# Recurrent stage of a hybrid decoder step: paired products in four quarters of the array, the next pair's preparation moved

## The reference, cut to what matters

```python
decay = jnp.exp(-jnp.exp(w_log))                       # w_log from tanh(xw) @ w_decay
a = jax.nn.sigmoid(a0 + xa @ w_aaa)
kk = k * k_k
k = k * (1.0 + (a - 1.0) * k_a)
kk = kk / jnp.maximum(jnp.sqrt(jnp.sum(kk * kk, axis=-1, keepdims=True)), 1e-12)
a_vec, b_vec = -kk, kk * a_h

def step(S, inp):
    r_t, w_t, k_t, v_t, av_t, bv_t = inp
    sa = jnp.einsum('bhvk,bhk->bhv', S, av_t)
    S = S * w_t[:, :, None, :] + sa[..., None] * bv_t[:, :, None, :] + v_t[..., None] * k_t[:, :, None, :]
    return S, jnp.einsum('bhvk,bhk->bhv', S, r_t)

out = (groupnorm(y) * lnx_w + lnx_b + bonus) * g       # bonus = sum(r * k * r_k) * v
```

## Time and profile before

| | us |
|---|---|
| median of 3 runs | 2424.03 (2423.95 to 2425.92) |
| profiled execution | 2424.27 |
| its span | 2422.6 |
| recurrent stage (550 to 1148 of the span), of it | 598 |
| TensorE busy there | 588.5 |
| VectorE busy there | 398.1 |
| ScalarE busy there | 193.1 |

### The profile page before, as it was taken

How to read it: one execution, slowest core, us unless ns; L and a number is a source line. 1 busy time by engine, 2 the same in 40 slices (tenths; PEclk the granted TensorE clock), 3 DMA queues, 4 the chain that set the end, 5 groups by cost and what they waited for, 6 DMA issues and landing times.

```text
span 2422.6 us, 48639 instructions
## 1 busy us (share of the span) xinstructions
PE 2375.1 (98%) x19616; PEld 2272.0 (94%) x19616; DVE 1461.7 (60%) x2052; ACT 895.2 (37%) x1040; POOL 131.4 (5%) x203
## 2 busy tenths in 40 slices
PE   8999999999999999999999998999999999999998
PEld 6899999898988889888999988999999999999998
DVE  5645544555677666776544446666666666666676
ACT  6443344343333333332434344333333333333334
POOL 3000001000000010000000001000000000000003
PEclk9999999999999999999999999999999999999999
DMA  7554487342333333323444632444444444444443
GB/s 267 185 162 145 156 290 244 104 141 83 96 98 95 93 126 100 97 86 95 142 150 151 202 121 89 158 154 139 156 156 140 154 150 144 140 158 153 152 143 110
DMA packets 282189, 346.67 MB, mean 143 GB/s; under 512 B 6957, under 2 KB 240733, under 8 KB 280907
## 3 DMA queue, kind: packets, MB, share of 16 engines
q1 hardware_dynamic: 271883, 307.66, 39.6%
q0 software_dynamic: 9712, 36.30, 4.5%
q10 hardware_dynamic: 464, 0.79, 0.1%
HBM read 333.83 MB, written 10.89 MB: 142 GB/s over the span
## 4 chain that ended last, share of the span: by engine, by line
PE 86%; DVE 8%; issue 3%; ACT 2%; DMA 1%; DVEq 0%; SPq 0%; ACTq 0%
PE bank L246 20%; PE bank L247 20%; PE bank L255 20%; PE bank L1165 5%; PE bank L227 4%; PE bank L228 4%; PE bank L229 4%; DVE work L906 1%; ACT hi L211 1%; DVE lo L218 1%; PE bank L1181 1%; PE bank L511 1%; DVE q L833 1%; PE bank L512 1%; PE bank L518 1%
## 5 line engine op out<-in xcount | busy, mean ns | idle before, releaser
L218 DVE TENSOR_TENSOR lo<-raw,hi 128x2048 fp32r<-128x2048 f32 x286 | 655.6, 2292 | 505.5 <-ACT hi L211 488.0
L246 PE MATMUL bank<-ah,hi 128*128 128x320 f32 x3200 | 958.0, 313 | 0.2 <-DVE al L532 0.2
L247 PE MATMUL bank<-al,hi 128*128 128x320 f32 x3200 | 945.8, 309 | 0.0
L211 ACT ACTIVATE hi<-raw 128x2048 fp32r<-128x2048 f32 x286 | 548.0, 1916 | 924.1 <-PE bank L255 675.4
L246 PEld LDWEIGHTS bank<-ah,hi 128*128 128x128 f32 x3200 | 600.7, 188 | 12.9 <-issue 9.8
L247 PEld LDWEIGHTS bank<-al,hi 128*128 128x128 f32 x3200 | 601.1, 188 | 0.4
L255 PE MATMUL bank<-ah,lo 128*128 128x320 f32 x3200 | 546.6, 311 | 0.0
L255 PEld LDWEIGHTS bank<-ah,lo 128*128 128x128 f32 x3200 | 486.4, 188 | 3.7 <-issue 0.8
L227 PE MATMUL bank<-bh,hi 128*128 128x320 f32 x704 | 218.7, 311 | 0.2 <-DVE work L2314 0.2
L229 PE MATMUL bank<-bh,lo 128*128 128x320 f32 x704 | 217.6, 309 | 0.0
L228 PE MATMUL bank<-bl,hi 128*128 128x320 f32 x704 | 217.5, 309 | 0.0
(11 more groups left out here) (377 smaller groups left out, 2035.7 us busy)
## 6 DMA issues: line engine op xcount, KB each, us to landing
raw<-in_w_in SPq DMA_DIRECT2D x98, 1024.0 KB, 5.3
raw<-in_w_up SPq DMA_DIRECT2D x88, 1024.0 KB, 5.1
raw<-in_w_down SPq DMA_DIRECT2D x44, 1024.0 KB, 5.1
raw<-in_w_branch SPq DMA_DIRECT2D x24, 1024.0 KB, 5.4
raw<-in_w_out SPq DMA_DIRECT2D x16, 1024.0 KB, 5.5
raw<-in_w_mem_k SPq DMA_DIRECT2D x8, 1024.0 KB, 5.5
raw<-in_w_mem_v SPq DMA_DIRECT2D x8, 1024.0 KB, 5.3
work<-in_cache_mem_k POOLq DMA_DIRECT2D x8, 1024.0 KB, 6.0
```

The costliest lines, as they stand in the source:

```text
L211: act.activation(hi[c % NS][:, :], raw[c % 2][:, :], ACT.Copy).then_inc(S("hi_done"), 1)
L218: dve.tensor_tensor(lo[c % NS][:, :], raw[c % 2][:, :], hi[c % NS][:, :], ALU.subtract)\
L246: pe.matmul(out, w, xh[:, 8 * h + k, :], start=h + k == 0, stop=False)
L247: pe.matmul(out, w, xl[:, 8 * h + k, :], start=False, stop=False)
```

## The change

- Products with inputs of both kinds are made two at a time in one pass over chunks (`both`): A with B, beT with Cb, Bk with Ck, vT with kaT. Chunks 0 and 1 (`TURNED`) send head 0 to partitions 64 to 127 and head 1 to 0 to 63, in one bank; chunks 2, 3 and 4 (`UPRIGHT`) stay, in a second bank. Their matmuls alternate. The products that follow read the turned halves through `out_of_chunk`.
- G and the first two terms of S0 to S3 become St and Ss, made together; S1 to S3 keep the one term with the state before, and VectorE adds the rest while it copies out. X is split in X1 and X. The terms of y of chunks 0 and 1 are made beside S4.
- bonus and ssq come first in the pair. bonus is copied out by ScalarE and multiplied later by VectorE; the root of ssq is taken by ScalarE from PSUM, and the bound on the norm becomes the `min` of `prepare_norm`. `prepare_kk` is done a pair ahead.
- z and za stand behind vks, ahead of RT2. On VectorE prepare_norm comes ahead of RT2, prepare_k behind it, prepare_logs behind Z1, branch(0, 1) behind the copy of y, weights_low(4) behind prepare_rest.
- `STEPS` puts the 48 branch steps in other places, and `HELD` replaces `Y_STEPS`: four are within alT, three ahead of y.

```diff
-        for _n in ["A", "bonus", "B", "beT", "Cb", "A2", "B2", "Bk", "vT", "RT1", "B4", "Ck", "kaT", "RT2", "s0t",
-                   "Q", "QT", "Z0", "Z0s", "Q2", "QT2", "XB", "Z1", "QT4", "alT", "Z2", "z", "za", "ssq", "Z3", "X4", "G",
-                   "S0", "S1", "S2", "S4", "S3", "X", "g", "mean", "trp", "var", "tr0", "tr1"]:
+        for _n in ["bonus", "ssq", "ABt", "ABs", "beCt", "beCs", "A2", "B2", "BCt", "BCs", "RT1", "B4", "vkt", "vks", "z", "za", "RT2", "s0t",
+                   "Q", "QT", "Z0", "Z0s", "Q2", "QT2", "XB", "Z1", "QT4", "alT", "Z2", "Z3", "X4", "St", "Ss",
+                   "S1", "X1", "S2", "S4", "S3", "X", "g", "mean", "trp", "var", "tr0", "tr1"]:
...
-        STEPS = {"A": 8, "A2": 3, "RT1": 3, "RT2": 3, "Q": 3, "XB": 3, "Z2": 4, "Z3": 4, "S0": 2, "S1": 2, "S2": 2, "S3": 1, "X": 2,
+        STEPS = {"bonus": 8, "A2": 3, "RT1": 3, "RT2": 3, "Q": 3, "XB": 3, "alT": 4, "Z3": 4, "S1": 3, "S2": 3, "S3": 3,
                  "g": 5, "mean": 2, "var": 1}
-        Y_STEPS = 3
+        HELD = {"alT": 4, "g": 3}
...
-                masked(t_ad, "A", m_ad)
-                ps("bonus")
-                tt(bon, pbank("bonus")[:, 0:T], row_(i + 16), ALU.mult, "ring_out")
-                masked(t_bd, "B", m_bd, None)
-                tt(c5(t_bo)[:, 0:NCK], c5(pbank("B")[:, 0:T])[:, 0:NCK], bmid(m_bo[:, :], NCK), ALU.mult, "ring_out")
-                ps("beT")
-                vv.do(dve.tensor_copy(zc3[:, :, 0:64], c5(pbank("beT")[:, 0:T])), "ring_out")
-                ps("Cb")
-                tt(zc3[:, :, 64:128], c5(pbank("Cb")[:, 0:T]), m_in[:, :, :], ALU.mult, "ring_out")
...
+                for name, cs in (("ABt", TURNED), ("ABs", UPRIGHT)):
+                    k, states = 64 * len(cs), tuple(c for c in cs if c < NCK)
+                    ps(name)
+                    part(t_ad, name, 0, cs, m_ad)
+                    part(t_bd, name, k, cs, m_bd)
+                    part(t_bo, name, k, states, m_bo, "ring_out")
+                for name, cs in (("beCt", TURNED), ("beCs", UPRIGHT)):
+                    k = 64 * len(cs)
+                    ps(name)
+                    vv.do(dve.tensor_copy(zc3[:, cs[0]:cs[-1] + 1, 0:64], c3(pbank(name)[:, 0:k])))
+                    tt(zc3[:, cs[0]:cs[-1] + 1, 64:128], c3(pbank(name)[:, k:2 * k]), m_in[:, cs[0]:cs[-1] + 1, :], ALU.mult, "ring_out")
...
+                dve.wait_ge(S("turned_out"), OUT0_A + N_OUT_A * i + OUT_A["bonus"] + 1)
+                tt(bon, bon, row_(i + 16), ALU.mult)
+                prepare_norm(dve, vv, i + 1)
                 plus(t_rt, "RT2")
-                prepare_kk(dve, vv, i + 1)
+                prepare_k(dve, vv, i + 1)
...
+                ps("X1")
+                tt(t_x[:, 64:128], t_x[:, 64:128], pbank("X1")[:, 0:64], ALU.add, "ring_out")
+                state(2)
                 branch(0, 0)
-                state(2)
                 weights_low(3)
                 ps("S4")
                 tt(sam, pbank("S4")[:, :].rearrange("p (b v) -> p b v", b=NB), s0t, ALU.add)
                 tt(sam, sam, bc(pend_s, HD), ALU.mult, "ring_out")
                 state(3)
-                branch(0, 1)
                 ps("X")
-                tt(t_x[:, 64:TP], t_x[:, 64:TP], pbank("X")[:, 0:192], ALU.add, "ring_out")
-                prepare_norm(dve, vv, i + 1)
-                weights_low(4)
+                tt(t_x[:, 128:TP], t_x[:, 128:TP], pbank("X")[:, 0:128], ALU.add, "ring_out")
                 prepare_al(dve, vv, i + 1)
                 dve.wait_ge(S("y_ps"), i + 1)
                 vv.do(dve.tensor_copy(y_, bank[6][:, 0:T]), "y_out")
+                branch(0, 1)
                 prepare_rest(dve, vv, i + 1)
+                weights_low(4)
...
+                ps("bonus")
+                act.wait_ge(S("gated_out"), j)
+                aa.do(act.activation(bon, pbank("bonus")[:, 0:T], ACT.Copy), "turned_out")
+                ps("ssq")
+                aa.do(act.activation(sq, pbank("ssq")[:, 0:T], ACT.Sqrt), "kk_root")
+                for name, c, k in (("vkt", 0, 128), ("vks", 128, 192)):
...
+            if ps:
+                ps("s0t")
+                aa.do(act.activation(qr[:, 896:1408], pbank("s0t")[:, :], ACT.Copy), "turned_out")
+                ps("alT")
+                aa.do(act.activation(alp_t[:, 0:192], pbank("alT")[:, 0:192], ACT.Copy), "turned_out")
             act.wait_ge(S("logs"), j + 1)
...
+                def into_chunk(o, a, b, c):
+                    for h in range(2):
+                        last = pe.matmul(o[half(h ^ (c in TURNED)), :], a[half(h), :], b[half(h), :], start=True, stop=True)
+                    return last
+                def out_of_chunk(o, a, b, c, start=True, stop=True, **kw):
+                    for h in range(2):
+                        r = half(h ^ (c in TURNED))
+                        last = pe.matmul(o[half(h), :], a[r, :], b[r, :], start=start, stop=stop, **kw)
+                    return last
+                def both(turned, upright, a1, b1, a2, b2):
+                    t, s = begin(turned), begin(upright, ahead=1)
+                    if turned == "ABt":
+                        wait("ops_ready", i + 1)
+                    def one(o, a, b, c, n):
+                        return into_chunk(ch(o, n), ch(a, c), m_id if b is None else ch(b, c), c)
+                    one(s, a1, b1, 2, 0)
+                    one(t, a1, b1, 0, 0)
+                    one(s, a1, b1, 3, 1)
+                    one(t, a1, b1, 1, 1)
+                    one(s, a1, b1, 4, 2)
+                    one(t, a2, b2, 0, 2)
+                    one(s, a2, b2, 2, 3)
+                    end(one(t, a2, b2, 1, 3))
+                    one(s, a2, b2, 3, 4)
+                    end(one(s, a2, b2, 4, 5))
...
+                o = begin("alT")
+                into_chunk(ch(o, 1), ch(alp, 2), m_id, 2)
+                into_chunk(ch(o, 2), ch(alp, 3), m_id, 3).then_inc(S("al_upright"), 1)
+                for _ in range(HELD["alT"]):
+                    next(steps, None)
+                wait("al_upright", i + 1)
+                end(into_chunk(ch(o, 0), ch(alp, 1), m_id, 1))
...
+                def from_zb(o, c):
+                    return out_of_chunk(o, zb(c), ch(t_x, c), c, stop=False)
+                def from_ka(o, c):
+                    return out_of_chunk(o, ch(ka_t, c), ch(v_t, c), c, start=False)
+                def from_al(o, c):
+                    return out_of_chunk(o, ch(alp_t, c - 1), zb(c), c)
...
+                y_terms(0, 0, start=True)
+                heads(o[:, :], [(zb(NCK), sam_)], stop=False)
+                y_terms(0, 1)
+                y_terms(1, 0)
+                y_terms(1, 1)
+                end(heads(o[:, :], [(ch(ka_t, NCK), vtm_)], start=False))
...
```

More of the change, by code:

```diff
@@ L783, in wkv_pool @@
             for j in range(KW):
[L785 removed]
+                pool.wait_ge(S("wkv_ps"), PS0 + NPR * j + PR["bonus"] + 1)
                 load_low(min(j + 1, KW - 1))
@@ L935, in wkv_dve @@
                 plain(t_b2, "B2")
-                masked(t_bk, "Bk", m_st)
+                for name, cs in (("BCt", TURNED), ("BCs", UPRIGHT)):
+                    ps(name)
+                    part(t_bk, name, 0, cs, m_st)
+                    part(t_ck, name, 64 * len(cs), cs, m_in, "ring_out")
                 weights_low(0)
@@ L1129, in wait, with begin @@
                     pe.wait_ge(S(name), value)
-                def begin(name, *needs):
+                def begin(name, *needs, ahead=0):
                     p = PR[name]
-                    assert p == done[0], name
-                    for _ in range(STEPS.get(p, 0) - (Y_STEPS if name == "g" else 0)):
+                    assert p == done[0] + ahead, name
+                    for _ in range(STEPS.get(p, 0) - HELD.get(name, 0)):
                         next(steps, None)
@@ L1146, in begin @@
                             wait("low_out", 2 * i + 3 + (before == "za"))
+                        elif before == "ssq":
+                            wait("kk_root", i + 2)
                         else:
@@ L1174, in each, with half @@
                     end(last)
-                def turned(name, src, chunks=range(NC)):
-                    o = begin(name)
-                    for n, c in enumerate(chunks):
-                        for h in range(2):
-                            r = slice(64 * h, 64 * h + 64)
-                            last = pe.matmul(o[r, 64 * n:64 * n + 64], src[r, 64 * c:64 * c + 64], m_id[r, :], start=True, stop=True)
-                    end(last)
+                def half(h):
+                    return slice(64 * h, 64 * h + 64)
+                def into_chunk(o, a, b, c):
[23 more added lines that the diff above has]
+                    end(one(s, a2, b2, 4, 5))
                 def zb(c):
@@ L1197, in apply @@
                     end(last)
-                o = begin("A")
-                wait("ops_ready", i + 1)
-                for c in range(NC):
-                    s = slice(64 * c, 64 * c + 64)
```

(37 more changed lines are left out.)

142 lines of the change are left out of this document (70 added, 72 removed).

## The result

| | before | after |
|---|---|---|
| median of 4 runs, us | 2424.45 (2423.95 to 2425.92) | 2440.72 (2439.24 to 2441.47) |
| profiled execution, us (its span) | 2424.27 (2422.6) | 2439.24 (2437.5) |
| ratio, 95% interval | | 1.0065 (1.0048 to 1.0083) |
| TensorE busy | 2375.1 | 2358.5 |
| mean granted clock | 0.997 | 0.993 |

The changed kernel is 0.65% slower. The forecast was 2429, 4.8 us over before, with a range to 2440. So the direction is that of the forecast's own sum, but the change is 16.3 us, over three times as large, and lies 0.7 us outside the range.

The account below looks back on a forecast made before the run. TensorE's queue order, with its waits for VectorE and ScalarE, was taken as the bound. Per pair, 4.1 us less work and 1.3 of old waits against 6.2 of new ones, walked as +0.60, times eight: 2424.3 + 4.8 = 2429 us, range 2414 to 2440.

Parts of the forecast that it names:

- the forecast's own sum: Per pair 76.91 us against 76.31, +0.60; times eight +4.8, giving 2429 us; chance 0.55.
- The large predicted waits: TensorE loses a pair: 1.77 us at beC (root), 0.31 at v/ka, 0.58 at St, 2.76 before var.
- those at BC and za: TensorE loses 0.16 us at BC waiting for A2's copy, 0.5 at za, which no longer runs beside z.
- rival B: Chunk products: quarters don't overlap, turned chunks cost 0.117 us each, 2.5 us a pair, 20 us: 2449; chance 0.13.
- rival A: Start of pair: root of ssq not in the way, 1.77 x 8 = 14.2 us less: 2415; chance 0.2.
- the wait before var: Behind y: VectorE's queue to the squares takes 8.4 us, TensorE's work 5.8, so var loses 2.76 us a pair.
- the term of the clock: Var to the next pair: taken as 1.41 + 7.21 us as before, nothing added for the clock.
- own range: Whole kernel: 0.5 us a pair reading error each way, 0.33 more if quarters start apart: 2424 to 2436.
- the walk: TensorE's queue through one pair, walked in order with its waits: 76.91 us against 76.31, +4.8 us over eight pairs.
- the move behind y: VectorE's branch(0,1) and low part behind y's copy: y's end to var 8.56 us, before 6.55.

Follow-up runs that it names:

- e3: Changed kernel with every chunk product in the two upright quarters, same order and banks: 2460.79 us, 1.0148 of before.
- e2: Changed kernel with ScalarE taking the root of ssq ahead of unit 0's high part: 2428.51 us, 1.0017 of before.
- e6: Changed kernel with four unread 128x320 products filling TensorE's wait before var: 2432.10 us, 1.0031 of before.
- e4: Kernel before with only branch(0, 1) and weights_low(4) moved behind VectorE's copy of y: 2440.45 us, 1.0063 of before.
- e1: Changed kernel with branch(0, 1) and weights_low(4) put ahead of VectorE's wait for y: 2411.36 us, 0.9945 of before.
- e8: Changed kernel with the moves of e1 and e2 together: 2403.75 us, 0.9908 of before.
- e9: e5 with VectorE making RT's sum behind A2's copy instead of ahead of it: 2396.47 us, 0.9885 of before.
- e10: Changed kernel with one more 128x320 product a pair ahead of the state's transposes: 2439.70 us, 1.0062 of before.
- e11: e4 with one more 128x320 product a pair ahead of the state's transposes: 2445.97 us, 1.0086 of before.
- e7: Changed kernel with branch(0, 1) alone ahead of y on VectorE, weights_low(4) staying behind: 2423.31 us, 0.9992 of before.
- e5: e8 with unit 2's high part allowed on ScalarE before its wait for the logs: 2397.36 us, 0.9884 of before.

## Why the prediction was right or wrong

**What held.** Times from the start of pair 2, predicted and then read: AB 1.21, 1.42; beC 3.72, 3.64; branch steps 4.56, 4.49; BC 8.77, 8.81; v/ka 13.92, 14.07; steps of RT2 16.1, 16.19; St 42.7, 42.94; y 57.7, 57.88; end of y 59.74, 59.96; var 68.3, 68.60. The large predicted waits stand at their places and with their releasers (root, v/ka, St, var); those at BC and za are too short for the list. A pair was to take 76.91 us and takes 77.22 where the clock holds. Against before that is +0.9 instead of +0.6. The 0.3 is the 68.60 for 68.3 of var: 0.2 of it stands at the end of y already, the rest is in VectorE's queue behind y. The 0.2 arose behind beC, mostly before v/ka (0.15 late) and St (0.24 late). AB was 0.21 late too, but that did not count, since the wait for the root took it up and beC started 0.08 early. At AB I had taken 0.05 from ScalarE's copy to TensorE, and the trace has 0.25 (628.01 to 628.26), while beC starts 0.05 behind its root. Why these two differ, no run tells.

**Four quarters (rival B).** e3 puts them at 20 us for 21 chunks a pair, so they overlap fully. That disproves B. It also goes, for this form, against the rule that was weighed there from "TensorE: Matmul & The Clock Gate" of the Trainium skill, Part 3: a turned chunk shares its rows with the upright one beside it and still costs nothing that the time shows. The distance of about 25 ns that the page's Part 1 gives for two matmuls is no bound across four quarters either: forty records start and end within 0.91 us, 23 ns each with the last one's end counted in.

**The root (rival A).** The high part did stand before it in every pair. But its price was not the full 1.77 us. The trace shows 1.31 of waiting, as AB started later and took longer than walked, and with the root ahead (e2) a pair wins 0.97, since BC's wait for A2's copy takes back about 0.5. The prediction took the price of A one for one, and so overstated A by this, because VectorE's queue behind the wait was not walked again without it.

**The clock, the step that failed.** The prediction priced the wait before var at its length: "var starts at 68.3; y's end to var is 8.56 us, of which 2.76 lost", and then "Var to the next pair is 1.41 + 7.21 as before". The second sentence is the wrong one. In five pairs TensorE gets 1.2 GHz behind that wait, and var to the next pair takes 1.63 us more. I had read the clock only as the mean of the stage, 1.00, where the longest waits of before are 0.7 us, and did not ask what a wait of 2.8 us does to it. So the term of the clock was put at nothing, and it measured 8.2 us in the profile; e6, with the wait filled, lies 8.6 us lower. Without the falls the kernel would lie at 2432, inside the own range of 2424 to 2436. The same page of the Trainium skill, in "HAM oscillation — how this bites in real kernels", describes a kernel in which the wait for a DMA between two bursts of matmuls throws TensorE back to the low clock each time. Its waits are drawn at about 3 to 5 us, longer than the 2.4 us here. This trace goes beyond that: waits of 2.4 us did it in five of eight pairs, and the 1.9 us near 472 did it in eight of thirteen profiles. A fall of the clock behind var's wait should have been a rival of its own, with a price from rows at the low clock.

**The terms.** The profiled run lies 10.2 us above the forecast of 2429. The clock is 8.2 of it. The other 2.0 are the walk: 6.8 us in the account above (5.7 in seven periods, 0.45 and 0.65 at the ends) for the 4.8 forecast. The median lies another 1.5 above the profiled run, which was the fastest of the four. One fall more in the others would fit (two of them have a mean clock of 0.992 for 0.993), but they have no trace, and it stays open. The largest single term, the move behind y, is confirmed in its direction and nearly in its size: I had reckoned 8.56 against 6.55, 2.0 us a pair; e4 has 2.1 in the kernel before, e1 2.6 in the changed one.

## What to carry to other kernels

Walk TensorE's queue by start times, and then walk it again for each wait that you would take away: a wait behind it on another engine is often nearly as late (e2, e8, e9). Work that a neighbouring engine can do while it waits for a result belongs ahead of that wait in its queue; moved behind, it delays everything that hangs on the result (2.6 us a pair here, and 29 us in all with what the clock added). Where a change leaves TensorE standing longer than any wait of the stage before, give the clock a term of its own; if the wait can't go, filler products can be cheaper than the fall (e6).

## What the runs showed of the hardware

- In the recurrent stage TensorE's granted clock went from 2.4 to 1.2 GHz only at waits of 2.4 us, between 0.5 us before the wait's end and 1.4 us behind it: in 5 of 8 pairs (changed kernel), 4 of 8 (e2, e10 and e11), 1 of 8 (e4) and 6 of 8 (e3). It did so in none where the stage's longest wait was 1.6 us (e7), 1.3 (e1) or less (e5, e8, e9), and in none where the wait was filled (e6). No length follows from this as a bound: ahead of the stage, a wait of 1.9 us was followed by a fall in eight of thirteen profiles. Each count is of one execution.
- One fall costs 1.63 us in the changed kernel, where eight transposes take 1.91 us instead of 1.04. It costs 1.0 in e2, where a wait further on takes up the rest.
- Four 64x64 quarters work at once in fp32, in pairs that share rows and pairs that share columns: 40 records in 0.91 us, against 1.38 in two quarters.
